# Up projection of a gated MLP: the weights become the stationary operand and 256 tokens move, so that the result has features on the partitions

## The reference

```
def conv_ffn(h, w_up, conv_w, conv_b, w_down):
    u = h @ w_up                                   # (256, 2048) @ (2048, 11008)
    up = jnp.pad(u, ((0, 0), (CONV_WIDTH - 1, 0), (0, 0)))
    uc = conv_b
    for i in range(CONV_WIDTH):
        uc = uc + up[:, i:i + S] * conv_w[i]       # along the tokens, a weight per feature
    gate, val = jnp.split(uc, 2, axis=-1)          # 5504 features each
    return (jax.nn.silu(gate) * val) @ w_down
```

## Time and profile before

| | us |
|---|---|
| median of 3 runs | 2297.28 (2296.43 to 2298.26) |
| the profiled execution | 2297.32 |
| its span, first to last instruction | 2295.5 |
| PE busy | 2162.0 (94%) |
| PE weight loads busy | 1805.4 (79%) |
| DVE busy | 1493.9 (65%) |
| ACT busy | 1051.8 (46%) |
| mean granted clock of TensorE | 0.978 |

### The profile page before, as it was taken

The page is one execution under the profiler, slowest core; times in us unless marked ns, Lnnn a source line. Parts: engine busy times, 40 slices in busy tenths (PEclk is TensorE's granted clock), DMA queues, the critical chain, the costliest instruction groups (busy, mean ns, idle before and its releaser), DMA issues.

```text
span 2295.5 us, 27603 instructions
## 1 busy us (share of the span) xinstructions
PE 2162.0 (94%) x10218; PEld 1805.4 (79%) x10218; DVE 1493.9 (65%) x2227; ACT 1051.8 (46%) x1569; POOL 140.9 (6%) x131
## 2 busy tenths in 40 slices
PE   4899996698999999998999999999999999999997
PEld 4778885576788778887888888888778998888876
DVE  5958886697676767756557575545457755455565
ACT  2233335544454445444445454444554544434553
POOL 0100001011100000000002021000000210000100
PEclk9989998898999999999999999999999999999999
DMA  9959990096667666755555555544445555444443
GB/s 357 392 218 367 366 365 28 15 356 225 211 228 249 209 204 210 247 165 173 192 189 185 178 164 163 185 129 147 149 141 188 162 168 191 145 147 148 157 170 114
DMA packets 241612, 458.84 MB, mean 200 GB/s; under 512 B 12542, under 2 KB 164300, under 8 KB 240972
## 3 DMA queue, kind: packets, MB, share of 16 engines
q1 hardware_dynamic: 241484, 457.10, 58.3%
HBM read 454.95 MB, written 2.10 MB: 199 GB/s over the span
## 4 chain that ended last, share of the span: by engine, by line
PE 74%; DVE 5%; ACT 3%; issue 2%; POOL 0%; DMA 0%; DVEq 0%; ACTq 0%; SPq 0%; POOLq 0%
PE PS L285 22%; PE PS L292 22%; PE PS L287 22%; PE PS L1079 2%; PE PS L1022 2%; DVE WLO L276 1%; PE PS L1199 1%; ACT WHI L268 1%; PE PS L1087 1%; DVE SPARE L370 1%; DVE BIG L1480 1%; PE PS L1094 0%; PE PS L1096 0%; PE PS L1095 0%; PE PS L926 0%
## 5 line engine op out<-in xcount | busy, mean ns | idle before, releaser
L285 PE MATMUL PS<-WHI,HH 128*128 128x512 f32 (+4 forms) x2680 | 1061.5, 396 | 35.3 <-ACT WHI L268 16.3
L276 DVE TENSOR_TENSOR WLO<-RAWT,WHI 128x1024 fp32r<-128x1024 f32 (+4 forms) x694 | 830.5, 1204 | 355.8 <-ACT WHI L268 355.7
L287 PE MATMUL PS<-WHI,HLO 128*128 128x512 f32 (+4 forms) x2680 | 1039.6, 388 | 2.0 <-issue 2.0
L268 ACT ACTIVATE WHI<-RAWT 128x1024 fp32r<-128x1024 f32 (+4 forms) x694 | 691.9, 1015 | 378.1 <-PE PS L292 315.2
L292 PE MATMUL PS<-WLO,HH 128*128 128x512 f32 (+4 forms) x2680 | 714.2, 389 | 3.1 <-DVE WLO L276 3.1
L285 PEld LDWEIGHTS PS<-WHI,HH 128*128 128x128 f32 x2680 | 508.3, 190 | 145.0 <-issue 25.4
L292 PEld LDWEIGHTS PS<-WLO,HH 128*128 128x128 f32 x2680 | 505.6, 189 | 103.2 <-DVE WLO L276 4.7
L287 PEld LDWEIGHTS PS<-WHI,HLO 128*128 128x128 f32 x2680 | 509.2, 190 | 96.0 <-issue 3.3
L370 DVE SCALAR_TENSOR_TENSOR AD<-AD,SM 128x1024 f32<-128x1024 f32 x83 | 110.4, 1330 | 10.1 <-DMA AD<-w_ada 8.2
L1124 ACT ACTIVATE WK<-PS 128x384 f32<-128x384 f32 x48 | 23.4, 487 | 194.4 <-PE PS L1087 194.4
L723 ACT ACTIVATE HH<-BIG 128x256 fp32r<-128x256 f32 x118 | 48.6, 412 | 108.3 <-PE PS L292 107.2
(11 more groups left out here) (277 smaller groups left out, 1478.2 us busy)
## 6 DMA issues: line engine op xcount, KB each, us to landing
RAWT<-w_up SPq DMA_DIRECT2D x168, 512.0 KB, 4.8
AD<-w_ada SPq DMA_DIRECT2D x152, 512.0 KB, 5.8
RAWT<-w_out SPq DMA_DIRECT2D x96, 512.0 KB, 4.5
RAWT<-w_in SPq DMA_DIRECT2D x48, 1024.0 KB, 5.1
RAWT<-w_down SPq DMA_DIRECT2D x86, 512.0 KB, 4.6
RAWT<-w_in SPq DMA_DIRECT2D x44, 992.0 KB, 7.9
RAWT<-w_in SPq DMA_DIRECT2D x40, 924.0 KB, 4.9
BIG<-w_ada SPq DMA_DIRECT2D x40, 512.0 KB, 11.1
```

What stands on the lines that cost most here:

```text
L268: act.activation(WHI[:, (q % HL) * GR:(q % HL) * GR + size], r, ACT.Copy).then_inc(S("hi_done"), 1)
L276: dve.tensor_tensor(WLO[:, (q % HL) * GR:(q % HL) * GR + size], r, h.bitcast(F32), ALU.subtract)\
L285: pe.matmul(o, lh, wh, start=first and bank not in seen, stop=False)
L287: pe.matmul(o, ll, wh, start=False, stop=False)
```

## The change

The up projection gets a PE function of its own, up_pe. The 128 x 128 stationary operand is now a tile of the weights (WHI or WLO), and the moving operand is HH or HLO with all 256 tokens. A full chunk has four feature tiles, each a half bank of PSUM. A group has 24 matmuls with 256 columns in place of 12 with 512. The result stands with features on the partitions, as the taps want it: the two copies to U, the eight transposes and the semaphore ff_turn are gone, and the taps read the products' own banks (0 to 3). The ACT tap moves from group 6 to group 4 and waits for mm_done; the DVE taps stay at 6. A chunk waits at its first group for the taps of the chunk two before (ff_conv), as does the down projection at its start for the last taps. DMAs, the splits of the weights, the taps, the SiLU and the gate product are the same instructions as before.

```diff
@@ place of the products
-        for name, slots, chunks in (("w_in", 44, 11), ("w_out", 16, 0), ("w_up", 88, 22), ("w_down", FT, 0)):
+        for name, slots, chunks in (("w_in", 44, 11), ("w_out", 16, 0), ("w_up", 88, 0), ("w_down", FT, 0)):
...
-        def ffn_tile(t):
-            return PS[:, 4 + t // 2, (t % 2) * T:(t % 2 + 1) * T]
+        def ffn_tile(par, t):
+            return PS[:, 2 * ((up.c0 + par) % 2) + t // 2, (t % 2) * T:(t % 2 + 1) * T]
+
+        def up_pe(pe, it, par, nt, stat=None, after=None, ada=None):
+            cn = it * 2 + par
+            for s in range(up.spc):
+                gs, reg = slot_of(up, it, par, s)
+                for j in range(2):
+                    q, gi = 2 * gs + j, 2 * s + j
+                    if gi == 0:
+                        ge(pe, S("ff_conv"), cn - 1)
+                    if stat is not None:
+                        pe.wait_ge(S("h_lo"), stat + gi + 1)
+                    tiles_ = [(k, t) for k in range(2) for t in range(2 * nt)]
+                    wt = {(k, t): slice((q % HL) * GR + (k * 2 * nt + t) * P, (q % HL) * GR + (k * 2 * nt + t + 1) * P)
+                          for k, t in tiles_}
+                    pe.wait_ge(S("hi_done"), reg * 2 + (q + 1))
+                    for k, t in tiles_:
+                        kt, o = 2 * gi + k, ffn_tile(par, t)
+                        pe.matmul(o, WHI[:, wt[k, t]], HHv[:, kt, :], start=kt == 0 and t % 2 == 0, stop=False)
+                        pe.matmul(o, WHI[:, wt[k, t]], HLv[:, kt, :], start=False, stop=False)
+                    pe.wait_ge(S("lo_done"), reg * 2 + (q + 1))
+                    for k, t in tiles_:
+                        kt = 2 * gi + k
+                        mm = pe.matmul(ffn_tile(par, t), WLO[:, wt[k, t]], HHv[:, kt, :], start=False,
+                                       stop=kt == KT - 1 and t % 2 == 1)
+                    mm.then_inc(S("mm_done"), 1)
...
-        def ffn_turn(pe, cn, nt):
-            pe.wait_ge(S("ev_act"), cn + (up.c0 + 1))
-            pe.wait_ge(S("ev_dve"), cn + (up.c0 + 1))
-            ge(pe, S("ff_conv"), cn * 1)
-            for t in range(2 * nt):
-                for h in range(2):
-                    mm = pe.transpose(ffn_tile(t)[:, h * P:(h + 1) * P], U[:, h, t * P:(t + 1) * P], ident)
-            mm.then_inc(S("ff_turn"), 1)
...
-            act.wait_ge(S("ff_turn"), cn + 1)
+            act.wait_ge(S("mm_done"), it * (4 * up.spc) + 2 * (up.g0 + up.spc * (par + 1)))
...
-                        chunk_pe(eng, up, it, par, n, stat if first else None,
-                                 first_hooks(who, prep) if first else
-                                 with_gate({2: lambda e: ffn_turn(e, pc, 2)}, cn), ada)
+                        up_pe(eng, it, par, 2 if n is None else 1, stat if first else None,
+                              first_hooks(who, prep) if first else with_gate({}, cn), ada)
...
-                            4: lambda e: chunk_out(e, up, pit, ppar, 0, dst=U[:, 0, :]),
-                            6: lambda e: ffn_act_tap2(e, pc, 2), 7: lambda e: ffn_act_silu(e, pc, 2)}, cn))
+                            4: lambda e: ffn_act_tap2(e, pit, ppar, 2), 7: lambda e: ffn_act_silu(e, pc, 2)}, cn))
...
-                            4: lambda e: chunk_out(e, up, pit, ppar, 1, dst=U[:, 1, :]),
-                            6: lambda e: ffn_dve_taps(e, pc, 2)}
+                            6: lambda e: ffn_dve_taps(e, pit, ppar, 2)}
...
-            pe.wait_ge(S("ev_act"), up.c0 + UPN)
-            pe.wait_ge(S("ev_dve"), up.c0 + UPN)
+            pe.wait_ge(S("ff_conv"), UPN)
```

More of the change, by code:

```diff
@@ L147, in build_program @@
         TAIL1 = BIG[:, 2 * W1:2 * W2]
-        U = TAIL[:, 0:1024].rearrange("p (h n) -> p h n", h=2)
         GROW = TAIL[:, 0:2048]
@@ L1184, in build_program @@
         up = prod["w_up"]
-        def ffn_tile(t):
-            return PS[:, 4 + t // 2, (t % 2) * T:(t % 2 + 1) * T]
+        def ffn_tile(par, t):
[24 more added lines that the diff above has]
+                    mm.then_inc(S("mm_done"), 1)
+                    if after and gi in after:
+                        after[gi](pe)
+                    if ada is not None and par == 1 and ada[1] == 3 and gi == 3:
+                        ada_reduce(pe, ada[0])
@@ L1202, in ffn_act_tap2 @@
-        def ffn_act_tap2(act, cn, nt):
-            act.wait_ge(S("ff_turn"), cn + 1)
+        def ffn_act_tap2(act, it, par, nt):
+            cn = it * 2 + par
+            act.wait_ge(S("mm_done"), it * (4 * up.spc) + 2 * (up.g0 + up.spc * (par + 1)))
             act.wait_ge(S("ff_wcol"), cn + 1)
@@ L1207, in ffn_act_tap2, with ffn_dve_taps @@
             for t in range(2 * nt):
-                op = act.activation(T1[:, t, :], ffn_tile(t), ACT.Identity, scale=ffn_w(3, t, nt),
+                op = act.activation(T1[:, t, :], ffn_tile(par, t), ACT.Identity, scale=ffn_w(3, t, nt),
                                     bias=ffn_w(0, t, nt))
             op.then_inc(S("ff_tap2"), 1)
-        def ffn_dve_taps(dve, cn, nt):
+        def ffn_dve_taps(dve, it, par, nt):
+            cn = it * 2 + par
             dve.wait_ge(S("ff_tap2"), cn + 1)
             for t in range(2 * nt):
-                op = dve.scalar_tensor_tensor(T1[:, t, 1:], ffn_tile(t)[:, 0:T - 1], ffn_w(2, t, nt),
+                op = dve.scalar_tensor_tensor(T1[:, t, 1:], ffn_tile(par, t)[:, 0:T - 1], ffn_w(2, t, nt),
                                               T1[:, t, 1:], ALU.mult, ALU.add)
@@ L1220, in ffn_dve_taps @@
             for t in range(2 * nt):
-                op = dve.scalar_tensor_tensor(T1[:, t, 2:], ffn_tile(t)[:, 0:T - 2], ffn_w(1, t, nt),
+                op = dve.scalar_tensor_tensor(T1[:, t, 2:], ffn_tile(par, t)[:, 0:T - 2], ffn_w(1, t, nt),
                                               T1[:, t, 2:], ALU.mult, ALU.add)
@@ L1317, in run_up @@
             if who == "act":
-                chunk_out(eng, up, 10, 1, 0, n=256, dst=U[:, 0, 0:256])
-                ffn_act_tap2(eng, 21, 1)
+                ffn_act_tap2(eng, 10, 1, 1)
                 ffn_act_silu(eng, 21, 1)
@@ L1322, in run_up @@
                 ffn_dve_gate(eng, 20, 2)
[L1323 to L1326, removed]
+                ffn_dve_taps(eng, 10, 1, 1)
             elif who == "pool":
@@ L2313, in _ @@
             run_up(pe, "pe", prep_turn("pe", None, None, ty), stat=ty.at("ts"))
-            pe.wait_ge(S("ev_act"), up.c0 + UPN)
-            pe.wait_ge(S("ev_dve"), up.c0 + UPN)
+            pe.wait_ge(S("ff_conv"), UPN)
             def banks_up(e):
-                e.wait_ge(S("ff_conv"), UPN)
                 e.wait_ge(S("gr_row"), 8)
```

## The result

The change makes the kernel faster: 2278.22 us median (2270.34 to 2279.65, 4 runs) against 2297.77 us (2296.43 to 2299.78, 4 runs), a ratio of 0.9907 with the interval 0.9883 to 0.9931. The forecast was 2290.3 us with a range of 2281.0 to 2299.5, so the gain came out at 19.5 us where 7.0 were forecast. The profiled execution took 2278.27 us, its span is 2276.5.

The account below looks back on a forecast made before the run. PE's time per up-projection chunk was taken as the bound, with ACT, DVE and DMAs having room. Chunks 1 to 20 -4.4, chunk 0 +0.3 and the end -2.9 summed to -7.0 us: 2290.3 us, range 2281 to 2299.5.

Parts of the forecast that it names:

- The transposes, 0.90 us a chunk: Up projection's full chunks: eight transposes and the return from them cost PE 0.90 us of a 22.86 us chunk.
- the end, -2.9: Chunk 21 to the down projection's start: transposes gone -0.9, wait for WLO of group 6 -0.8, earlier tap -1.2 us.
- Chunk 0, +0.3: Chunk 0: groups 3 to 6 hide longer matmuls behind waits for POOL; the other four groups cost +0.3 us.
- 192 matmuls at 0.1179 us, 22.64 us a chunk: Chunks 1 to 20: new-form distance taken from chunk 21; chunk 0.22 us shorter than 22.86, -4.4 us in all.
- The lower end that I had put down, 0.1144: Chunks 1 to 20: price in proportion to columns, half of 0.2288 us; chunk of 21.96 us, -18.0 us in all.
- Rival C: Up projection: repeated stationary tile makes the second load cheap, distance 0.1144 us, 2276.6 us in all; chance 0.12.
- Rival A: Up projection: new form's distance grows as loads have little cover; 0.1203 us gives 2299.5, 0.1225 gives 2307.9; chance 0.12.
- Rival B: PE's instruction reads in the loop: 16 more, each costing 2.03 us, +32 us to 2323; chance 0.04.
- What hides the tap at ACT's group 4, the DVE taps and the wait on ff_conv: Up-projection loop: these cost nothing; WHI and WLO splits finish before PE wants them, ff_conv has 10 us of room.

Follow-up runs that it names:

- e7: Kernel before the change, each 512-column up-projection product in full chunks issued as two of 256, tokens still stationary, transposes and copies kept: 2309.37 us, ratio 1.0056.
- e12: Looped changed kernel with idle fp32r products, operand roles swapped (HH/HLO tiles stationary, WHI/WLO columns moving), result not right: 2293.96 us, one execution.
- e2: Changed kernel with each group's HH products first, then its HLO products, so no two matmuls in a row share a stationary tile: 2276.87 us, ratio 0.9926.
- e4: Changed kernel plus eight idle fp32 transposes of a constant behind group 2 of chunks 1 to 21: 2304.83 us, ratio 1.0033.
- e5: Changed kernel plus eight idle 128-column fp32r products a chunk, in place of eight idle transposes: 2293.37 us, ratio 0.9981.
- e10: Changed kernel plus three idle 128-column fp32r products in eight places (chunk 1, loop's first chunk, behind reductions and gate rows): 2275.72 us, ratio 0.9903.
- e1: Changed kernel run again, nothing altered: 2276.79 us (2275.28 to 2286.66, 6 runs), ratio 0.9931.
- e6: Changed kernel plus one idle fp32 transpose of a constant behind group 2 of chunks 1 to 20: 2286.21 us, one run.
- e8: Changed kernel with the hardware loop over chunks 2 to 17 written out, one gate-vector semaphore count adapted: 2277.04 us, ratio 0.9907.
- e9: Kernel before with products as two of 256 columns, tokens stationary, plus four idle fp32r products behind the transposes in chunks 1 to 19: 2319.89 us, ratio 1.0095.
- e3: Changed kernel with the old 512-column products, tokens stationary; transposes and copies gone, result not turned, so not the reference's: 2273.04 us, ratio 0.9898.

## Why the prediction was wrong

- **The transposes, 0.90 us a chunk, and the end, -2.9:** right. The kernel without transposes and with old products moved 25.3 us, 21 by these terms; chunk 21 and the end measured -3.1.
- **Chunk 0, +0.3:** measured +0.2.
- **192 matmuls at 0.1179 us, 22.64 us a chunk:** this is the step that failed, a term mis-sized: "I take 0.1179, since it is the row of the same shape, engine state and stretch". It was the same shape, but not the same state: two distances exist for it, and the operands of rows 4 had the other roles, with which the long one is the rule (e7, e12). Measured 0.1133 us and 21.76 us in some 130 of 160 groups, where the forecast had 0.1179: 130 x 0.11 = 14 us of the 15 that were missed. The lower end that I had put down, 0.1144, did not reach it either: two half-size matmuls take 226.7 ns, 2 ns less than one whole. The sign of the gain was right, and so were its other terms.
- **The warning was in the earlier trace rows:** one form at 2.745 and at 2.80 us. I used it only upwards, as a rival, and took the one row of the new shape as its normal state. A form with two speeds in one trace asks for both as ends.
- **Rival C:** the time that came, by a mechanism that does not exist (e2). **Rival A:** its distance of 0.1203 us did not appear with weights stationary and activations moving. **Rival B:** no gap inside the loop at the doubled rate, but the turn costs 4.4 us more than with the old products without transposes, 7.22 and 4.44 against 2.87 and 4.43. The kernel with the loop written out has none of it.
- **What hides the tap at ACT's group 4, the DVE taps and the wait on ff_conv:** right, PE has no wait in the loop but the turn.
- **Pages:** by the Trainium skill's TensorE: Matmul & The Clock Gate (Back-to-back issue gap) two 256-column matmuls should cost 2.5 ns more than one of 512; the rows show 7 more at 117.9 ns and 2 less at 113.3. The share of LDWEIGHTS, by which the Trainium skill's page Perfetto Trace Analysis (Identifying the Most-Contended Engine) judges how near PE is to its limit, is full here, 180.00 of 180.00 us, and the matmuls still came at the shortest distance measured for this form.

What stays open is what sets the distance. That the product in a break matters is shown by e4 against e5 and by e10, that the roles matter for how often each distance holds by e7 and e12. But plain waits change it too (e1, e5, e6), the old roles reach 113 ns in chunk 0 (e7), and an fp32 product can't be told from one that reads the constants. So neither is the whole cause, and a cause inside the engine was not isolated. Nor was an execution of 2286 us profiled, so that it began at 2.83 us is a guess, if one that e8's profile makes likely.

## What to carry to other kernels

Read the price of a matmul from the distance of starts in more than one stretch, and take a second speed of one form as a bound in both directions, not as noise. Turn a product so that its result needs no transpose: the transposes and copies were the gain here, 25 us with 4.6 at the loop's turn, and the form of the products alone was worth nothing. Fp32 products inside a stream of fp32r products can cost more than their own time. With the weights stationary, a few 128-column fp32r products behind them, 0.4 us, mostly bring the faster distance back; with the tokens stationary they did not (e9, e12). In the looped kernel this gained nothing beyond the spread, and with the loop written out 6 us (2277.04 to 2270.94, with intervals of the ratio that overlap).

## What the runs showed of the hardware that was not expected

- A stream of fp32r matmuls of 128 x 128 over 256 columns at full clock ran at 113.3, 117.9 or 120 ns a matmul, depending on the operands' pairing and on what came before; 512 columns at 228.8 or 233.3 ns.
- An fp32 product in between (16 of one column, one transpose, a gate row) can change the distance, to either side and for as long as 62 groups (e8). A plain wait of 1 us in chunk 0 did so too, from 114 to 118 ns in e6.
- The turn of the hardware loop costs PE from 1.8 us (e3: two groups of 7.3 us in place of 5.5) to 6.8 (e5: 12.4 in place of 5.6), for nearly the same body. Where PE idled 1.3 us there (e3), the granted clock stayed at 1.00; where it idled 4.2 to 4.3 us (after, before), the clock behind it was 0.50 to 0.54.
